# Strassen's seven down products in another order, all sums of weights on VectorE, and two w_ada buffers

## The reference

```python
h2 = rms_norm(x, norm2[l])
x = x + jnp.square(jax.nn.relu(h2 @ w_up[l])) @ w_down[l]
```

```python
mod = c @ w_ada[l] + b_ada[l]
shift, scale, gate = jnp.split(mod, 3, axis=-1)
h = rmsnorm(x, norm_g[l]) * (1.0 + scale[:, None]) + shift[:, None]
```

## Time and profile before

| | us |
|---|---|
| median of 3 runs | 1884.39 (1882.36 to 1886.46) |
| profiled execution, its own time | 1883.6 |
| its span, first to last instruction | 1881.8 |
| TensorE busy | 1773.1 (94% of the span) |
| VectorE busy | 1130.0 (60%) |
| ScalarE busy | 816.4 (43%) |
| GpSimd busy | 658.0 (35%) |
| mean granted TensorE clock | 0.981 |

### The profile page before, as it was taken

One profiled execution on the slowest core, in us unless ns is written; L12 is line 12 of the kernel. 1 busy time (PEld: TensorE's weight loads), 2 busy tenths in 40 slices (PEclk: granted clock), 3 DMA queues, 4 the chain that ended last, 5 costly groups with the idle time before them and its releaser, 6 DMA issues.

```text
span 1881.8 us, 22625 instructions
## 1 busy us (share of the span) xinstructions
PE 1773.1 (94%) x8863; PEld 1436.2 (76%) x8865; DVE 1130.0 (60%) x1644; ACT 816.4 (43%) x1498; POOL 658.0 (35%) x296
## 2 busy tenths in 40 slices
PE   9999899899989899998996898989899999999998
PEld 8687668787878686876785686867679888888786
DVE  4678753747575757787426676767741224329467
ACT  5544644544343555345444252525444443344212
POOL 4242434333333242424342333424144334334443
PEclk9999999999999999999998899999899999999999
DMA  7224003241423141210024425251243122322221
GB/s 226 68 71 165 11 22 103 68 134 49 131 67 112 45 130 60 90 45 23 24 87 127 156 90 163 83 177 58 90 152 96 62 89 75 128 67 90 90 68 45
DMA packets 107409, 171.24 MB, mean 91 GB/s; under 512 B 21999, under 2 KB 39815, under 8 KB 107176
## 3 DMA queue, kind: packets, MB, share of 16 engines
q1 hardware_dynamic: 106264, 169.79, 28.0%
q10 hardware_dynamic: 1040, 0.00, 0.0%
HBM read 166.56 MB, written 7.93 MB: 93 GB/s over the span
## 4 chain that ended last, share of the span: by engine, by line
PE 78%; DVE 15%; issue 3%; ACT 2%; DMA 1%; POOL 1%; SPq 1%; DVEq 0%; ACTq 0%
PE G L2621 18%; PE G L2623 18%; PE G L2622 18%; PE S L2621 4%; PE S L2622 4%; PE S L2623 4%; DVE w_lo L2487 2%; PE S L2909 2%; DVE s_low L2479 1%; PE S L1340 1%; DVE X L2516 1%; DVE hidden L2454 1%; DVE select L2330 1%; DVE work L2166 1%; DVE neg_max L2366 1%
## 5 line engine op out<-in xcount | busy, mean ns | idle before, releaser
L1612 POOL TENSOR_TENSOR w_lo<-raw,w_hi 128x1024 fp32r<-128x1024 f32 (+2 forms) x140 | 335.3, 2417 | 638.2 <-ACT w_hi L1689 330.1
L2621 PE MATMUL G<-h_hi,w_hi 128*128 128x512 f32 x896 | 356.2, 398 | 2.6 <-DVE h_lo L1092 1.9
L2623 PE MATMUL G<-h_hi,w_lo 128*128 128x512 f32 x896 | 350.0, 391 | 0.0
L2622 PE MATMUL G<-h_lo,w_hi 128*128 128x512 f32 x896 | 349.5, 390 | 0.0
L2621 PE MATMUL G<-w_hi,h_hi 128*128 128x512 f32 (+2 forms) x704 | 277.3, 394 | 2.2 <-DVE h_lo L2119 1.2
L2623 PE MATMUL G<-w_hi,h_lo 128*128 128x512 f32 (+2 forms) x704 | 267.1, 379 | 0.0
L2622 PE MATMUL G<-w_lo,h_hi 128*128 128x512 f32 (+2 forms) x704 | 266.7, 379 | 0.0
L1747 ACT ACTIVATE w_hi<-raw 128x1024 fp32r<-128x1024 f32 x140 | 144.3, 1052 | 269.8 <-PE G L2623 152.4
L1647 POOL TENSOR_TENSOR w_lo<-raw,w_hi 128x1024 fp32r<-128x1024 f32 x52 | 135.7, 2627 | 251.2 <-ACT w_hi L1747 251.2
L2621 PEld LDWEIGHTS G<-h_hi,w_hi 128*128 128x128 f32 x896 | 168.5, 188 | 41.2 <-issue 4.4
L2623 PEld LDWEIGHTS G<-h_hi,w_lo 128*128 128x128 f32 x896 | 168.5, 188 | 36.0
(11 more groups left out here) (357 smaller groups left out, 2990.8 us busy)
## 6 DMA issues: line engine op xcount, KB each, us to landing
raw<-in_w_in_dram SPq DMA_DIRECT2D x40, 1024.0 KB, 5.3
raw<-in_w_up_dram SPq DMA_DIRECT2D x26, 1024.0 KB, 5.3
raw<-in_w_down_dram SPq DMA_DIRECT2D x26, 1024.0 KB, 5.0
raw<-in_w_out_dram SPq DMA_DIRECT2D x12, 1024.0 KB, 4.9
w_ada<-in_w_ada_dram SPq DMA_DIRECT2D x24, 512.0 KB, 3.7
raw_more<-in_w_down_dram SPq DMA_DIRECT2D x6, 1024.0 KB, 5.0
raw_more<-in_w_up_dram SPq DMA_DIRECT2D x6, 1024.0 KB, 5.2
skew_scratch<-line_scratch SPq DMA_DIRECT2D x1, 4608.0 KB
```

Of the source, the lines that this page charges most:

```text
L1612: ins = pool.tensor_tensor(w_lo[:, c % SPLIT_SLOTS, part, 0:n], raw[:, raw_slot(l, c), part, 0:n], w_hi[:, c % SPLIT_SLOTS, part, 0:n].bit ...
L2621: pe.matmul(dst, a_hi, b_hi, start=first, stop=False, skip_group_check=more)
L2622: pe.matmul(dst, a_hi, b_lo, start=False, stop=False, skip_group_check=more)
L2623: return pe.matmul(dst, a_lo, b_hi, start=False, stop=last, skip_group_check=more)
```

## The change

The products S3 and S1 change places; the two bank pairs are then used in turn. The second of the next group's up halves, U1, moves behind S4. U0's slot is now B11's (T1's place) and U3's is T2's. T1 and T4 are made by VectorE, T1 in `before_products`, T4 behind the weights of S3, and GpSimd's `weights_sum` goes. VectorE's list and ScalarE's are in another order. The scaling of rows in layer 1's group 3 moves out of `take_sum` into `scale_rows`, called after both takes. w_ada has two buffers, each with its semaphore; a load waits for the part two before it, and the first two for nothing. The second_params move behind all loads of layer 1's FFN and wait until the last part of w_ada is added. Of the diff, the core:

```diff
-PRODUCTS = (("A11", "B11"), ("A12", "B21"), ("S2", "T2"), ("S3", "T3"), ("S1", "T1"), ("S4", "B22"), ("A22", "T4"))
+PRODUCTS = (("A11", "B11"), ("A12", "B21"), ("S2", "T2"), ("S1", "T1"), ("S3", "T3"), ("S4", "B22"), ("A22", "T4"))
 NP = len(PRODUCTS)
-P_A11, P_A12, P_S2, P_S3, P_S1, P_S4, P_A22 = range(NP)
-LONG_BANK = (True, False, True, True, False, False, True)
-READ_BEFORE = (P_A22, P_S4, P_A11, P_S2, P_A12, P_S1, P_S3)
-GOES_TO = ((0, 1, None), (0, 1, P_A11), (0, 0, None), (1, 0, None), (1, 0, P_S3), (0, 0, P_S2), (1, 1, None))
+P_A11, P_A12, P_S2, P_S1, P_S3, P_S4, P_A22 = range(NP)
+LONG_BANK = (True, False, True, False, True, False, True)
+READ_BEFORE = (P_A22, P_S4, P_A11, P_A12, P_S2, P_S1, P_S3)
+GOES_TO = ((0, 1, None), (0, 1, P_A11), (0, 0, None), (1, 0, None), (1, 0, P_S1), (0, 0, P_S2), (1, 1, None))
...
-                order += {P_S3: [("U", g + 1, 0)], P_S1: [("U", g + 1, 1)],
+                order += {P_S3: [("U", g + 1, 0)], P_S4: [("U", g + 1, 1)],
...
-        orders.append([at["T2"], at["B12"], at["B11"], at["B21"]])
+        orders.append([at["B11"], at["T2"], at["B12"], at["B21"]])
...
-    return RAW_ORDER[l][n] if g == 0 else role_slot(l, g - 1, ("T2", "B12", "T2", "B11")[n])
+    return RAW_ORDER[l][n] if g == 0 else role_slot(l, g - 1, ("B11", "B12", "B11", "T2")[n])
...
                     for n in itertools.islice(ada_parts, count):
-                        sp.wait_ge(ada_free, n + 1)
                         k, at = n // 3, D_MODEL * (n % 3)
-                        sp.dma_start(w_ada[:], A["w_ada_2"][0, P * k:P * k + P, at:at + D_MODEL]).then_inc(ada_loaded, 16)
+                        if n >= 2:
+                            sp.wait_ge(ada_free, n - 1)
...
-                load_modulation(1)
+                load_modulation(2)
                 wait_up_split(sp, l, 0, 0)
                 load_down(0, "B12")
                 wait_up_split(sp, l, 0, 1)
                 load_down(0, "B22")
-                if l == DEPTH - 1:
-                    second_params(sp)
                 load_modulation(2)
                 wait_up_split(sp, l, 0, 2)
                 load_down(0, "B21")
-                load_modulation(4)
+                load_modulation(3)
                 for g in range(1, FFN_GROUPS):
                     sums = 2 * (l * FFN_GROUPS + g)
-                    wait_product_split(sp, l, g - 1, P_S2)
-                    sp.wait_ge(sum_made["T1"], sums)
-                    sp.wait_ge(sum_made["T4"], sums)
+                    wait_product_split(sp, l, g - 1, P_S1)
                     load_up(g, 0)
+                    load_modulation(1)
                     wait_product_split(sp, l, g - 1, P_S3)
                     load_up(g, 1)
                     load_modulation(1)
                     wait_up_split(sp, l, g, 0)
                     load_up(g, 2)
-                    wait_product_split(sp, l, g - 1, P_S1)
-                    load_up(g, 3)
-                    load_modulation(3)
-                    wait_up_split(sp, l, g, 1)
-                    load_down(g, "B11")
                     wait_product_split(sp, l, g - 1, P_S4)
                     load_down(g, "B12")
                     load_modulation(1)
+                    sp.wait_ge(sum_made["T1"], sums)
+                    sp.wait_ge(sum_made["T4"], sums)
+                    load_up(g, 3)
+                    wait_up_split(sp, l, g, 1)
+                    load_down(g, "B11")
+                    load_modulation(1)
                     wait_product_split(sp, l, g - 1, P_A22)
                     load_down(g, "B22")
-                    wait_up_split(sp, l, g, 2)
+                    load_modulation(1)
+                    wait_up_split(sp, l, g, 3)
                     load_down(g, "B21")
                     load_modulation(1)
+                if l == DEPTH - 1:
+                    sp.wait_ge(ada_ready, 1)
+                    second_params(sp)
...
-                    wait_product_split(pool, l, g, P_A11)
-                    weights_sum(g, "T1", role_slot(l, g, "B22"), role_slot(l, g, "B11"), t2_half)
-                    wait_product_split(pool, l, g, P_A12)
-                    weights_sum(g, "T4", role_slot(l, g, "B21"), role_slot(l, g, "B21"), t2_half)
...
                     weight_half(at(P_A12), 0)
                     block_high(g, "A12", 1)
+                    block_high(g, "S2", 1)
                     weight_half(at(P_A12), 1)
-                    block_high(g, "S2", 1)
                     weight_high(at(P_S2))
+                    block_high(g, "S1")
+                    weight_high(at(P_S1))
                     block_high(g, "A22")
-                    block_high(g, "S1")
-                    weight_high(at(P_S3))
+                    weight_half(at(P_S3), 0)
                     block_high(g, "S4")
+                    weight_half(at(P_S3), 1)
                     if more:
                         up = lambda n: FFN_AT["U", g + 1, n]
                         weight_high(up(0))
-                        weight_high(at(P_S1))
+                        weight_high(at(P_S4))
                         weight_high(up(1))
-                        weight_high(at(P_S4))
-                        for t in range(TT):
+                        weight_high(at(P_A22))
+                        for t in range(3):
                             up_tile(g + 1, 0, t)
-                        weight_high(at(P_A22))
                         weight_high(up(2))
+                        up_tile(g + 1, 0, 3)
                         first_blocks_high(g + 1)
                         weight_high(up(3))
                         second_blocks_high(g + 1)
...
+                def scale_rows(g, p):
+                    if not last or g < FFN_GROUPS - 1:
+                        return
...
+                def sum_of_weights(g, name, role, minuend):
+                    for hh in range(2):
+                        part = slice(2 * hh, 2 * hh + 2)
...
+                def sum_t1(g):
+                    wait_product_split(dve, l, g, P_A11)
+                    sum_of_weights(g, "T1", "B11", "B22")
+                def sum_t4(g):
+                    wait_product_split(dve, l, g, P_A12)
+                    sum_of_weights(g, "T4", "B21", "B21")
                 def before_products(g):
...
+                    sum_t1(g)
 ...
                     weight_low(g, P_A12, 1)
+                    sum_s4(g)
+                    block_low(g, "S2", 0)
+                    block_low(g, "S2", 1)
+                    weight_low(g, P_S2, 0)
                     take_sum(g, P_A11, 0)
-                    sum_s4(g)
+                    weight_low(g, P_S2, 1)
                     take_sum(g, P_A11, 1)
-                    block_low(g, "S2", 0)
-                    weight_low(g, P_S2, 0)
-                    block_low(g, "S2", 1)
-                    weight_low(g, P_S2, 1)
+                    block_low(g, "S1")
+                    weight_low(g, P_S1, 0)
                     take_sum(g, P_A12, 0)
+                    weight_low(g, P_S1, 1)
+                    take_sum(g, P_A12, 1)
+                    take_sum(g, P_S2, 0)
+                    take_sum(g, P_S2, 1)
                     weight_low(g, P_S3, 0)
-                    take_sum(g, P_A12, 1)
                     weight_low(g, P_S3, 1)
+                    sum_t4(g)
+                    scale_rows(g, P_A12)
+                    block_low(g, "S4")
                     block_low(g, "A22")
                     if more:
                         add_modulation(1)
-                    block_low(g, "S1")
-                    block_low(g, "S4")
-                    take_sum(g, P_S2, 0)
-                    if not more:
-                        weight_low(g, P_S1, 0)
-                    take_sum(g, P_S2, 1)
-                    if not more:
-                        weight_low(g, P_S1, 1)
+                    take_sum(g, P_S1, 0)
+                    take_sum(g, P_S1, 1)
+                    weight_low(g, P_S4, 0)
                     take_sum(g, P_S3, 0)
-                    weight_low(g, P_S4 if not more else P_S1, 0)
                     take_sum(g, P_S3, 1)
-                    weight_low(g, P_S4 if not more else P_S1, 1)
+                    weight_low(g, P_S4, 1)
                     if more:
-                        add_modulation(3)
-                        weight_low(g, P_S4, 0)
-                    take_sum(g, P_S1, 0)
-                    if not more:
-                        weight_low(g, P_A22, 0)
-                    take_sum(g, P_S1, 1)
-                    if not more:
-                        weight_low(g, P_A22, 1)
-                    if more:
-                        weight_low(g, P_S4, 1)
-                        add_modulation(1)
-                        for hh in range(2):
-                            sum_s3(g + 1, hh)
-                        for hh in range(2):
-                            weight_low(g, P_A22, hh)
+                        add_modulation(2)
```

(59 more changed lines are left out.)

7 lines of the change are left out of this document (3 added, 4 removed).

## The result

The changed kernel takes **1805.0 us** (median of 4 runs, 1804.9 to 1805.8) beside 1883.6 for the kernel before (4 runs): ratio 0.9582, 95% interval 0.9565 to 0.9598. Faster by 78.6 us, where the forecast of 1792 meant some 92. The number lies inside the range given, but 2 us above the forecast's own range (1788 to 1803). The profiled execution took 1805.02, its span is 1803.2.

What follows compares the result with a forecast made beforehand. TensorE's waits on lower weights and bank takes lose 95.9 us in the FFN stages. 1883.6 − 95.9 + 0.8 + 1.4 + 1.2 = 1791.1, forecast 1792 us against the median; own range 1788 to 1803, full range 1787 to 1816.

Steps and rivals of the forecast that it cites:

- Banks in turn: FFN products: order S2, S1, S3, S4 rests each PSUM bank pair one product, 5.44 us, for VectorE's take.
- VectorE's list: VectorE's new order of work in each FFN group: every entry in time, A11's second take by only 0.3 us.
- hand-over: Tight timing of VectorE's list in each group: 0.1 us a group kept as loss, 0.8 in all.
- The walk: Count of VectorE's list from a group's A11 start, products back to back, setting each entry's finish against its due time.
- Sums on VectorE: T1 and T4 add 4.6 us a group, unstretched operations return 4.7; no path cost except layer 1's group 3.
- The start of layer 1: Two w_ada buffers and later parameters remove the 13.02 us wait before A11; with banks in turn, all 30.0 us go.
- The last S4: Layer 1's group 3, without up halves: S4 due at 27.2, its weights done at 28.6, +1.4 us.
- U0's split: GpSimd splits U0's weights in 5.24 us, to 27.5 after A11's start; second half needed at 28.56, in time by 1 us.
- rival (b): U0 becomes the wait: 2 us late in six groups, half losing clock, 17 us, giving 1809; chance 0.09.
- U1 and U2: Up halves one product after their predecessor: loading 6.5 us, needed after 6.8; three small idles charged, +1.2 us.
- The end of a layer: Both takes of a product come before its two scalings; VectorE's sum equal, charged 0, ends −0.7 and +0.7.

Runs made afterwards that it cites:

- the two added subtractions: Changed kernel with two more 128x1024 subtractions per group on VectorE ahead of S2's weights: 1826.27 us, ratio 0.9696.
- T4 held: Changed kernel with VectorE waiting, ahead of its T4 sum, until GpSimd has split U0's weights: 1796.41 us, ratio 0.9531.
- T4 held and the parts moved: Changed kernel with T4 waiting for GpSimd's split of U0, and two modulation parts moved behind A22's w_lo, which is not held: 1793.22 us, ratio 0.9523.
- both holds: Changed kernel with T4 held until U0 is split, A22's weights until U1 is split, two modulation parts moved behind them: 1795.34 us, ratio 0.9527.
- the last group reordered: Changed kernel with each layer's last group reordered on VectorE: S4's weights earlier, A22's scaling in halves, nothing held: 1804.68 us, ratio 0.9581.

## Why the prediction was right, and where it was off

**Banks in turn: right.** No product waits for a take, and the clock stays at 1.00. **VectorE's list: right to 0.1 us.** From A11's start the second take of A11 ends at 11.85 (forecast 11.9), S3's weights at 20.15 (20.2), and S4's sum takes 1.22 us instead of 2.99. Charged 0.8 for the hand-over, found 0. The walk gave S2's start a margin of 0.8 us (A11's first take at 10.1, due 10.88); the two added subtractions showed 0.7. **Sums on VectorE: right**; put back, they cost 33 us. **The start of layer 1: right**, with less room than the walk had: A11 follows U3 directly, with its lower weights done 2.8 us ahead (978.65 + 2.35 = 981.0, due at 983.81) instead of the 5 to 7 of the walk. The single buffer alone brings 6.7 us of wait back. **The last S4:** charged 1.4, found 1.05 idle and 1.2 with the restart.

**The step that failed is U0's split: "GpSimd two halves in 5.24 us to 27.5 … in time by 1 us".** Everything ahead of it was as forecast: load issued at 15.94 (16.0), with ScalarE at 21.2 (21.2). But the split took 7.94 and ended at 30.28, due at 28.56. The term was 0 and is six times 1.90 us (a group in layer 0 takes 83.52 us, with T4 held 81.62): **11.4 us**. Layer 1 fits this: 282.9 us of matmuls, half of the 11.4 and 1.2 for S4 make 289.8, and its products take 289.97 (83.50 + 206.47). This is rival (b), at two thirds of its price, since no clock was lost with it. Its mechanism was put almost rightly: not T4 lies under the split but the two blocks, a w_lo and more behind it. The row for 5.24 was itself a split with little beside it; I moved VectorE's work next to it and kept the old duration. The same argument that removed GpSimd's sums (two engines stretch each other) had to be turned round: GpSimd is stretched by VectorE.

The lengths fit a rule. The Trainium skill (SBUF — State Buffer, SBUF: two separate sides) says that VectorE and GpSimd share a pair of ports as an exclusive lock, which the one that starts first holds for its whole instruction, VectorE when both its inputs come from SBUF. The trace agrees: the first half's 4.63 us is its own 2.4 and the 2.27 from 457.95 to 460.22, in which the two blocks run; the takes, which read PSUM, add nothing. That the back-to-back subtractions never let GpSimd in between is what these rows add.

**U1 and U2:** charged 1.2, found 0 in the changed kernel. With U0's wait gone, though, U1 waited in layer 1, so a part of this margin was U0's lateness. **The end of a layer:** charged 0 (±0.7), found +1.7 behind layer 1. Of this 0.9 lie ahead of the second block's first product (8.71 us behind A22, 1273.78 to 1282.49, where the kernel before took 7.78, 1354.09 to 1361.87); the other 0.8 come later and stay open. VectorE's scaling lies under GpSimd's next split there, and ScalarE waits 0.47 us for it:

```profile
1272.48 5.14 POOL L1617 TENSOR_TENSOR w_lo<-raw,w_hi 128x1024 fp32r<-128x1024 f32 x2 [52.62 <-ACT w_hi L1680]
...
1274.65 3.53 DVE L2523 TENSOR_TENSOR xn<-X,gain_row 128x512 f32<-128x512 f32 x2
...
1278.21 0.63 ACT L910 ACTIVATE relu<-xn 128x512 f32<-128x512 f32 x1 [0.47 <-DVE xn L2523]
```

Moving that scaling took this wait away and gained nothing, as ScalarE's own squares are late next. **Between the layers:** +2.2 us that no step had; see the last section.

**The account.** Profiled 1805.0 against 1791.1 summed: 11.4 (U0) + 2.2 + 1.7 − 1.2 (U1, U2) − 0.8 (hand-over) − 0.2 (S4) = 13.1 of 13.9 us; 0.8 is not assigned. Without the U0 term the time would be near the version with T4 held and the parts moved, 1793.2, beside the 1792 forecast.

## What to carry to other kernels

A duration read from a row holds only with the same neighbour on the other engine: when work is moved from GpSimd to VectorE, write down again what runs beside every remaining GpSimd instruction, in both directions. Where a split on GpSimd has a due time, let VectorE idle or do work on PSUM until it is through; a wait of 5 to 7 us per group on VectorE was worth 9 to 12 us in all here. And a gap closed on one engine's list should be followed to the next engine before it is counted (U0's went on to U1 and U3, S4's to ScalarE).

## What the runs showed of the hardware beyond that

VectorE stands idle for 1.9 us before one small operation of the attention (rows_b), with no cause in the profile. It occurs once in the changed kernel, in layer 1; with both holds once in layer 0; in three of the versions twice; in the kernel before and in the one with the last group reordered not at all. The changed kernel's row, then that of the two holds:

```profile
811.50 0.29 DVE L2301 TENSOR_TENSOR rows_b<-S,inv_sum 128x128 f32<-128x128 f32 x1 [1.90 <-issue]
```

```profile
182.19 0.29 DVE L2301 TENSOR_TENSOR rows_b<-S,inv_sum 128x128 f32<-128x128 f32 x1 [1.89 <-issue]
```

The code there is the same in all of them. Between the layers it makes 1.4 of the 2.2 us: from the first matmul with a weight behind layer 0's products to layer 1's A11 the changed kernel takes 340.5 us (643.29 to 983.81), and two versions that do not have the idle there, both holds and the last group reordered, take 339.1. The version with one w_ada buffer is one of those with two, so part of its 1.4 us above the expected range can be this. The two places, 1.9 us each, are also of the size by which single runs of one version differ (1791.8 to 1796.3), but only one run of each version has a trace. Why it moves was not tried and stays open.
